# A fifth buffer for expert weights in a decoder layer, with the final norm's factors loaded after the overflow tiles

## What is computed

```
h = rmsnorm(x, norm_ffn)
grp = argmax(h @ w_grp + b_grp)                    # 1 of 4 groups
top_val, top_idx = top_k(logits of that group, 2)  # 2 of its 8 experts
gate = softmax(top_val) * probability of the group
for e in range(32):                                # D_EXPERT = 256
    a, u = h @ w_e_gate[e], h @ w_e_up[e]
    out += (silu(a) * u * gate[:, e]) @ w_e_down[e]
x = x + out
return rmsnorm(x, norm_final)
```

## Time and profile before

| | |
|---|---|
| median of three runs | 1322.23 us (1320.62 to 1324.27) |
| the profiled execution | 1332.08 us |
| its span, first to last instruction | 1330.2 us |
| TensorE busy | 1153.4 us (87%) |
| VectorE busy | 607.1 us (46%) |
| ScalarE busy | 386.8 us (29%) |
| GpSimd busy | 205.6 us (15%) |
| moved by DMA | 252.06 MB, 189 GB/s on the mean |
| tiles 0 to 33 on TensorE | 929.89 to 1279.77 us |
| end, from the last down product | 50 us |

### The profile page before, as it was taken

One profiled execution on the slowest core, in us unless ns is written; L12 is line 12 of the kernel. 1 busy time (PEld: TensorE's weight loads), 2 busy tenths in 40 slices (PEclk: granted clock), 3 DMA queues, 4 the chain that ended last, 5 costly groups with the idle time before them and its releaser, 6 DMA issues.

```text
span 1330.2 us, 29623 instructions
## 1 busy us (share of the span) xinstructions
PE 1153.4 (87%) x12072; PEld 933.3 (70%) x12072; DVE 607.1 (46%) x1574; ACT 386.8 (29%) x686; POOL 205.6 (15%) x450
## 2 busy tenths in 40 slices
PE   1899999998797999999989989992999899999940
PEld 1889788776576877788867668882777676777720
DVE  3420245324375667765666542336334333433328
ACT  5221112222254455544565622320111111111103
POOL 3020000000211111211163210010111111111024
PEclk9899999999698799999988889995899999999975
DMA  7111654262647355544343433309399999999847
GB/s 297 41 39 42 226 184 151 95 190 108 131 97 225 72 123 123 115 105 113 92 134 106 138 143 115 103 37 363 131 363 389 377 378 361 379 382 367 329 141 275
DMA packets 69540, 252.06 MB, mean 189 GB/s; under 512 B 22208, under 2 KB 30304, under 8 KB 59552
## 3 DMA queue, kind: packets, MB, share of 16 engines
q1 hardware_dynamic: 59488, 220.03, 49.5%
q0 software_dynamic: 6112, 16.79, 3.8%
q10 hardware_dynamic: 3808, 13.37, 2.7%
HBM read 205.83 MB, written 49.15 MB: 192 GB/s over the span
## 4 chain that ended last, share of the span: by engine, by line
PE 71%; DMA 11%; DVE 10%; issue 4%; SPq 2%; ACT 1%; POOL 1%; DVEq 0%; POOLq 0%; ACTq 0%
PE PS L1936 12%; PE PS L1664 11%; PE PS L1811 9%; PE PS L1944 7%; PE PS L1876 7%; PE PS L1653 5%; DMA wdn<-in_wdn 5%; PE PS L1755 4%; PE PS L1791 4%; PE PS L1792 3%; DMA k<-T_d 2%; PE PS L1927 2%; DMA q<-shr 2%; PE PS L1785 2%; DMA wst<-in_wt 1%
## 5 line engine op out<-in xcount | busy, mean ns | idle before, releaser
L1006 ACT ACTIVATE pt<-PS,cst 128x512 f32<-128x512 f32 (+3 forms) x288 | 172.6, 650 | 183.3 <-PE PS L1792 140.9
L1936 PEld LDWEIGHTS PS<-XT,wgu 128*64 128x64 f32 x4352 | 184.4, 139 | 39.3 <-issue 38.2
L1936 PE MATMUL PS<-XT,wgu 128*64 128x96 f32 x4352 | 191.5, 249 | 12.5 <-issue 7.9
L1298 DVE CUSTOM_DVE_ANT_0 junkm<-PS,cst 128x512 f32<-128x512 f32 (+3 forms) x276 | 137.4, 533 | 110.3 <-PE PS L1755 107.2
L1811 PEld LDWEIGHTS PS<-V,pt 128*64 128x64 f32 x3840 | 138.8, 149 | 36.5 <-issue 22.8
L1811 PE MATMUL PS<-V,pt 128*64 128x65 f32 x3840 | 163.0, 239 | 0.0
L1944 PE MATMUL PS<-wdn,aT 128*96 128x512 f32 x272 | 122.5, 593 | 0.9 <-DVE YO L1577 0.9
L1755 PE MATMUL PS<-k,q 128*128 128x128 f32 (+3 forms) x336 | 98.4, 372 | 20.6 <-DMA k<-T_d 12.3
L776 POOL TENSOR_SCALAR_AFFINE_SELECT pt<-pt 128x128 f32<-128x128 f32 x224 | 68.1, 306 | 284.0 <-ACT pt L1006 235.8
L1664 PE MATMUL PS<-hTh,wth 128*128 128x512 f32 x256 | 102.5, 400 | 3.9 <-DVE wtl L1148 3.9
L1791 PE MATMUL PS<-q,k 128*128 128x512 f32 (+1 forms) x240 | 96.2, 408 | 6.4 <-DMA q<-shr 6.4
(11 more groups left out here) (252 smaller groups left out, 1695.6 us busy)
## 6 DMA issues: line engine op xcount, KB each, us to landing
wgu<-in_wgu SPq DMA_DIRECT2D x34, 2048.0 KB, 12.0
wdn<-in_wdn SPq DMA_DIRECT2D x34, 1024.0 KB, 18.7
q<-T_d SPq DMA_DIRECT2D x60, 256.0 KB, 4.6
k<-T_d SPq DMA_DIRECT2D x60, 256.0 KB, 5.6
Y_d<-YO ACTq DMA_DIRECT2D x34, 384.0 KB, 10.1
wst<-in_wt SPq DMA_DIRECT2D x16, 512.0 KB, 6.7
T_d<-thi SPq DMA_DIRECT2D x16, 512.0 KB, 2.7
T_d<-tlo SPq DMA_DIRECT2D x16, 512.0 KB, 3.9
```

What stands on the lines that cost most here:

```text
L1006: ins = nc.scalar.activation(pt[:, (n + 2) % 6, 0:nt * P], PS[:, n % 4, 0:nt * P], ACT.Exp, scale=C("slopes", h, h + 1), bias=C("kb", w, w ...
L1298: V_.tensor_tensor_reduce(out=junk_[:, n % 2, 0:L], in0=PS[:, bank, 0:L], in1=tab, scale=1.0, scalar=-3e38, op0=ALU.add, op1=ALU.max, accu ...
L1936: ins = mm(PS[h * HD:(h + 1) * HD, 2 + p, f * CAP:(f + 1) * CAP], wgu[q][:, c, lo:lo + HD], XT[:, p, c, :], start=(c == 0 and f == 0), sto ...
```

## The change

A constant RING = 5 takes the place of the 4 in the buffer's number and in the semaphores. The fifth pair of buffers lies in ZC, 24 KB a partition, over the routing tables. `ge`, `gd` and `aT`, which lay there, move to where `in_row` was.

SP waits in addition for the first gather (`xg_in[0]`) and loads expert 4 at once; from expert 5 on, a load waits for the down product of tile n - 5.

`gfin` and `junk3` lie in XT's place, so that `gfin` can be loaded only when the overflow tiles are done. Its load moves from ahead of load 4 to behind SP's overflow loop and a wait for `ovf_y`. VectorE's wait for it stays where it was.

```diff
+RING = 5
@@
-        ge = at("ge", [P, 2 * CAP], f32, ZC)
-        gd = at("gd", [P, 2 * CAP], f32, ZC + KB)
-        aT = at("aT", [P, 2, 2, CAP], f32, ZC + 4 * KB)
+        ge = at("ge", [P, 2 * CAP], f32, ZE + 24 * KB)
+        gd = at("gd", [P, 2 * CAP], f32, ZE + 25 * KB)
+        aT = at("aT", [P, 2, 2, CAP], f32, ZE + 26 * KB)
         wgu = [at(f"wgu{q}", [P, KC, 2 * DE], f32, o)
-               for q, o in enumerate((ZE + 8 * KB, ZD, ZD + 24 * KB, ZB + 32 * KB))]
+               for q, o in enumerate((ZE + 8 * KB, ZD, ZD + 24 * KB, ZB + 32 * KB, ZC))]
         wdn = [at(f"wdn{q}", [P, 2, D], f32, o)
-               for q, o in enumerate((ZE, ZD + 16 * KB, ZD + 40 * KB, ZB + 48 * KB))]
+               for q, o in enumerate((ZE, ZD + 16 * KB, ZD + 40 * KB, ZB + 48 * KB, ZC + 16 * KB))]
-        gfin = at("gfin", [P, D], f32, ZC + 12 * KB)
-        junk3 = at("junk3", [P, D], f32, ZC + 16 * KB)
+        gfin = at("gfin", [P, D], f32, ZB + 56 * KB)
+        junk3 = at("junk3", [P, D], f32, ZB + 60 * KB)
@@
             sp_.wait_ge(dve_did, DV.of("info"))
-            sp_.dma_start(gfin[:], a["g_fin"]).then_inc(gfin_in, 16)
-            for n in range(4, NE):
-                sp_.wait_ge(m_dn, n - 3)
-                load_expert(n, n % 4)
+            sp_.wait_ge(xg_in[0], 16)
+            load_expert(4, 4)
+            for n in range(RING, NE):
+                sp_.wait_ge(m_dn, n - RING + 1)
+                load_expert(n, n % RING)
             for n in range(NE, NB):
                 eid = sp_.value_load(info[0:1, 1 + n - NE:2 + n - NE], min_val=0, max_val=NE - 1)
-                sp_.wait_ge(m_dn, n - 3)
-                load_expert(eid, n % 4)
+                sp_.wait_ge(m_dn, n - RING + 1)
+                load_expert(eid, n % RING)
             sp_.wait_ge(m_dn, NB)
@@ behind SP's overflow loop
+            sp_.wait_ge(ovf_y, 16 * n_ovf + 1)
+            sp_.dma_start(gfin[:], a["g_fin"]).then_inc(gfin_in, 16)
             for t in range(NT):
                 sp_.wait_ge(k_out, t + 1)
@@ on TensorE
-                pe_.wait_ge(we_in[n % 4], 32 * (n // 4 + 1))
-                up_product(n % 2, n % 4).then_inc(m_gu, 1)
+                pe_.wait_ge(we_in[n % RING], 32 * (n // RING + 1))
+                up_product(n % 2, n % RING).then_inc(m_gu, 1)
@@
-                down_product(n % 2, n % 4).then_inc(m_dn, 1)
+                down_product(n % 2, n % RING).then_inc(m_dn, 1)
```

More of the change, by code:

```diff
@@ L436, in program @@
         h_st = [sem(f"h_st{p}") for p in range(2)]
-        we_in = [sem(f"we_in{q}") for q in range(4)]
+        we_in = [sem(f"we_in{q}") for q in range(RING)]
         idx_c = sem("idx_c")
```

## The result

The changed kernel takes 1315.64 us (median of eleven runs, 1308.65 to 1320.64) against 1322.23 before (eleven runs, 1320.62 to 1333.00, with the profiled one, 1332.08, as the second slowest). The medians differ by 6.6 us and the means, 1314.8 and 1324.2, by 9.4. The ratio on record, an estimate over all runs and not the quotient of the medians, is 0.9925, interval 0.9902 to 0.9948, that is 6.9 to 13.0 us less. So the size of the gain is known to a few us only; that there is one is clear of the noise. The forecast was "within 0.3%" at 1321.3 us: the time is inside the range of 1314.8 to 1327.2, but the kernel is faster, and I had given that one chance in five.

What follows compares the result with a forecast made beforehand. DMA and TensorE were both taken as nearly full in the expert loop, a walk through empty trips behind it. Terms -1.3 - 3.8 + 4.2 = -0.9 us gave 1321.3 us against the median 1322.23; range 1314.8 to 1327.2.

Steps and rivals of the forecast that it cites:

- First gather: Ahead of the expert loop: without gfin's load beside it, TensorE's wait falls from 8.0 to about 6.7 us; gain 1.3.
- Fifth buffer: Expert loop: load 4 goes out earlier into idle DMA time, so all six waits for weights go; gain 3.8 us.
- gaps in mid-product: TensorE stops inside expert products, taken for late instruction fetches behind full DMA queues; left at 6.3 us, bounds 0 and 12.6.
- rival (c): Expert loop: fetch gaps grow by the 3.8 us the waits gave up, sum +2.9, 1325.1 us; chance 0.08.
- my 10.2 against 9.68 us a tile: Expert loop: DMA's estimated time a tile against TensorE's undisturbed time; each tile eats about 0.5 us of the buffers' lead.
- rival (b): Expert loop: the fetch gaps vanish along with the waits, sum -7.2, 1315.0 us; chance 0.09.
- gfin at the end: Tail: gfin's load, behind SP's 19 empty trips, lands late and delays VectorE's first final sum; cost 4.2 us.
- my upper row of 6.2: Tail: upper bound in us for gfin's landing, the median of the final gathers; 4.9 was forecast.
- Rival (a): Tail: SP's empty trips are cheaper than VectorE's, gfin is hidden and costs 0; sum -5.1, 1317.1 us; chance 0.12.
- Moved scratch tiles: Scratch tiles at new addresses: same instructions, same sizes, so no effect on the time.
- The two rules: Skill rules: queues taken in turn (gfin's landing 5.0 us); fetch crossings mostly hidden, which the forecast called contradicted by 6.3 us.
- theory L: Experiments' theory: gain comes from first gather, DMA's lead and gfin at the end; the profiled pair's earlier difference is chance.

Runs made afterwards that it cites:

- e4: Kernel before with four buffers, only gfin's load moved behind SP's overflow loop; ratio 1.0036 (1.0008 to 1.0063).
- e0_before: Kernel before, unchanged, profiled once beside the experiments; expert tiles 352.9 us, tail 63.8 us.
- e10_before: Kernel before, unchanged, one more trace for the spread; expert tiles 355.1 us, tail 64.6 us.
- e1_after: Changed kernel run again, unchanged (also written e1); 1330.81 us against 1339.34 for the kernel before, ratio 0.9934.
- e11_after: Changed kernel, unchanged, one more trace for the spread (also written e11); expert tiles 343.1 us, tail 67.4 us.
- e8: Changed kernel, but load 4 and all later loads wait as with four buffers, so the fifth gives no lead; expert tiles 349.8 us.
- e3: Changed kernel with VectorE's wait for gfin moved to just ahead of the first product with gfin; ratio 0.9903 against the kernel before.
- e5: Changed kernel with gfin in a place of its own and loaded right behind load 4; ratio 0.9925 against the kernel before.
- e9: On top of e5, every engine steps over the overflow loop when no overflow tile exists; 1318.24 us against 1340.98 for the kernel before, ratio 0.9855.
- e7: Changed kernel with three buffers instead of five; 1425.41 us, expert tiles 437.1 us.
- e6: Changed kernel, loading only 16 of wdn's 128 partitions from expert 10 to 31, so DMA has less to move; expert tiles 340.7 us.

## Why the prediction was wrong, point by point

**First gather: right.** 8.0 fell to 6.8, predicted 6.7. The other traces have 7.9 and 8.7 before, 6.9 twice after, and e4 shows that it is gfin's load alone.

**Fifth buffer: right mechanism, wrong size. This is the step that failed.** I counted 3.8 us, all waits for weights in one trace, and left the gaps in mid-product as they were. Three traces of each kernel give:

| us | before | e0_before | e10_before | after | e1_after | e11_after |
|---|---|---|---|---|---|---|
| waits for weights | 3.8 | 4.8 | 6.9 | 0 | 0 | 0 |
| gaps in mid-product | 6.3 | 6.5 | 7.4 | 4.2 | 3.2 | 3.7 |
| first transposes to last down product | 349.9 | 352.9 | 355.1 | 344.0 | 342.6 | 343.1 |

The means are 352.6 and 343.2: the term is -9.4, not -3.8, with -5.9 in the trace pair of the result. (e4 and e8, with the old times, have 350.2 and 349.8; e3, e5 and e9, with the lead, 342.6, 343.9 and 343.7; by these the term is -6.7.) Of the 9.4, 5.2 are the waits for weights, where I had 3.8; 3.0 are the gaps, 6.7 down to 3.7, which I had left at 6.3; 1.2 are neither (a third of a fall of the clock in e0_before that cost 1.65 us is 0.5 of it). In the trace pair of the result it is 3.8 and 2.1 and nothing else, so the term I had put at nothing, the gaps, failed even there. I had written down the right reading, in rival (c): DMA sets the end of the loop in the kernel before. The sum didn't use it. Where a rate is the bound, the waits of one execution are not the stock that can be won: waits and gaps share the deficit, and their sum, 10.1, 11.3 and 14.3 here, is what lies open. Of it 3.2 to 4.5 stay as gaps in the six traces with the lead. The other side of the same point is the rate: my 10.2 against 9.68 us a tile, over the 30 loads behind the first four, is a deficit of some 15 us, of which the old lead covers a part, and that bound would have told me that 3.8 was low.

**Gaps: not constant.** My rival (b) had them vanish, and (c) had them grow. They shrank by nearly a half, at the same matmuls of the same tiles (10, 11 and 17 to 19): 6.3 to 7.4 us in the five traces with the old times of the loads, 3.2 to 4.5 in the six with the lead. The first two, 1.86 and 1.49 before, are 0.88 and 1.27 after; e8 has 1.64 and 1.27 with the old times. Why they are shorter when the wall has begun a load earlier isn't settled.

**gfin at the end: right in kind, forecast at twice its size.** +2.1 for +4.2. SP needs 0.50 us a trip and not VectorE's 0.70 (10.2 us instead of 14.0), and the landing is 6.6 instead of 4.9, above my upper row of 6.2. So -3.8 in the walk and +1.7 in the landing; that they partly cancel is luck. Rival (a) wanted the whole walk within 9.8 us (0.52 a trip) at a landing of 4.9; SP took 10.2 with entry and exit, which alone would have left 0.3, and the rest of the 2.1 is the longer landing. Under the conditions of the experiments it is +3.2 (67.4 against 64.2).

**Moved scratch tiles: right**, by e8 (one trace): with them moved and the old times of the loads the tiles take 349.8 us.

**The two rules.** gfin took 6.6 us beside the gathers and 3.6 in the mixed stretch; where it was issued when the gathers were nearly through (e1, e3, e4, e8, e11) it took 3.6 to 4.1. The estimate of 5.0 by the turn-taking of queues (the Trainium skill, DMA: Bandwidth & Descriptors, section Queues, rings and completion order) had the sign and was low: it gave gfin half of the flow, and in the trace its 0.52 MB are a quarter of the 2.20 MB that move while it is under way. Gaps in mid-product came to 3 to 7 us a run behind full queues and to none where DMA had room, in e7 and the later part of e6. That crossing into the next block of instructions is mostly hidden (the Trainium skill, Runtime: NRT & Kernel Launch, section Instruction fetch mechanics) holds here by count, with six gaps for 39 packets in the kernel before. I had called it contradicted; what the traces add is the part that isn't hidden while the queues are full.

**The base: one profiled execution.** The prediction stood on a trace 9.85 us above the median, and I named that as its weakness. The danger I saw was on the wrong side: the waits for weights are larger in the other two traces, not smaller. The first gather is issued at 924.2, 913.5 and 916.3 us in the traces of the kernel before and at 907.2, 919.1 and 913.5 in those of the changed one: the same code, up to 17 us apart, with no order in it. In all thirteen traces it lies between 907.2 and 924.2, with a mean of 916.9 in the four with four buffers and of 914.8 in the eight with five. The granted clock goes along: among the eleven runs of the changed kernel it is 0.932 in the quickest (1308.65) and 0.921 in the slowest (1320.64), and from 600 to 700 us of the profiled pair it is 0.93 before and 1.00 after. So theory L holds for that stretch: the 17.0 of the 22.1 us of the profiled pair are spread. An effect of 2 or 3 us there wouldn't show in it.

**The sum.** With the mean terms: -1.3 (first gather) - 9.4 (tiles) + 2.1 (tail) = -8.6 against a measured -9.9 (6.9 to 13.0 us less), and with +3.2 for the tail -7.5 against e1's -8.8 (5.5 to 12.0). Both lie within the intervals. With the smaller tile term, -6.7, the first sum is -5.9: below that interval, close to the 6.6 between the medians. The runs don't decide between the two. The chance was misplaced rather than the range: a case "waits and gaps together, 6 us more than one trace shows" was missing, between the forecast and (b).

## What to carry to other kernels

When DMA and an engine run at nearly the same pace, price a buffer by the rates and the lead, not by the waits that one trace shows; and look at how many loads the ring keeps under way, since below that number a buffer is worth ten times as much (87 us against 7 to 9 here, a good third of it by the clock that TensorE loses behind each long wait). A load that is moved behind a loop inherits the loop's empty trips and its neighbours' traffic: put the wait for it where the data is used, or give it a hole in the DMA time, as e5 does. Before costing anything, ask of the profiled execution where it stands among the runs.

## What the runs showed of the hardware that was not expected

- TensorE stops in mid-stream for 0.2 to 2.3 us at some of the packets of its instruction queue while the DMA engines are full, and at none at shares up to 0.89 (e6, 200 us of the expert stage). Each of 59 stops ends 2.5 to 3.1 us behind the start of such a packet of 16 KB.
- A wait of 2.8 to 5.3 us for weights is followed by 3 to 6 us of TensorE at a granted clock of 0.50 (1.2 GHz), all 16 times in e7. Of the 29 shorter waits for weights, up to 2.13 us, in the five traces with the old times of the loads one is.
- An empty trip of a loop with one condition inside costs 0.50 us on SP and 0.70 on VectorE; in the traces of the experiments single steps of it took 0.70 us for a stretch of 17 to 21 us, on both engines. What brings that about is open.
- A 512 KB load took 3.6 us in a mixed stretch, 6.6 beside the final gathers, 3.6 to 4.1 near their end, and 12.6 in e5, queued behind load 4.
